# Memory laid out transposed, multiplied before it is normalised, in the opening of an encoder block on one core

## The reference, cut to what matters

```python
h = rms_norm(x, norm_mix_pre)               # 512 x 1024
z = h @ w_in                                # k, v, q, qx, pin, gates
mkv = rms_norm(mem, norm_mem) @ w_mem_kv    # 256 x 1024 @ 1024 x 1024
mk, mv = split(mkv)                         # keys and values, 4 heads of 128 columns each
ox = memory_attention(qx, mk, mv)
# rms_norm(x, g) = x * rsqrt(mean(x*x) + 1e-6) * g
```

## Time and profile before

| | before |
|---|---|
| median of 3 runs | 829.38 us (828.52 to 830.69) |
| span of the profiled execution | 827.4 us |
| granted TensorE clock, mean | 0.996 |
| instructions | 10167 |
| busy: PE / DVE / ACT / POOL | 816.6 / 353.0 / 304.7 / 40.0 us |

### The profile page before, as it was taken

The page is one execution under the profiler, slowest core; times in us unless marked ns, Lnnn a source line. Parts: engine busy times, 40 slices in busy tenths (PEclk is TensorE's granted clock), DMA queues, the critical chain, the costliest instruction groups (busy, mean ns, idle before and its releaser), DMA issues.

```text
span 827.4 us, 10167 instructions
## 1 busy us (share of the span) xinstructions
PE 816.6 (99%) x3952; PEld 673.3 (81%) x3952; DVE 353.0 (43%) x516; ACT 304.7 (37%) x574; POOL 40.0 (5%) x96
## 2 busy tenths in 40 slices
PE   7999999999999999999999999999999999999997
PEld 6988777777788888888888988888888888888885
DVE  4742565566344522525655443333333333522122
ACT  5742555555445324334334242233222332412110
POOL 1100000243000000000001000000000000000000
PEclk9999999999999999999999999999999999999999
DMA  9543221311311333334271133333322232622011
GB/s 322 168 129 109 74 79 52 103 52 51 103 51 51 103 102 103 101 102 147 107 254 52 51 102 102 101 101 101 97 82 82 93 126 102 244 80 84 1 51 51
DMA packets 67782, 84.16 MB, mean 102 GB/s; under 512 B 3217, under 2 KB 61089, under 8 KB 67746
## 3 DMA queue, kind: packets, MB, share of 16 engines
q1 hardware_dynamic: 67712, 83.65, 30.9%
q10 hardware_dynamic: 34, 0.01, 0.0%
HBM read 81.54 MB, written 2.11 MB: 101 GB/s over the span
## 4 chain that ended last, share of the span: by engine, by line
PE 97%; DMA 1%; DVE 1%; ACT 0%; issue 0%; SPq 0%; DVEq 0%; POOLq 0%; POOL 0%; ACTq 0%
PE pair L988 90%; PE pair L1079 1%; PE pair L1062 1%; PE pair L1089 1%; PE pair L994 1%; PE pair L1069 1%; PE pair L1093 1%; DMA g_mem_b<-in_norm_mem 1%; PE pair L1015 0%; DVE mem_in L738 0%; PE pair L1110 0%; DVE wo_lo L351 0%; ACT wo_hi L346 0%; PE pair L1100 0%; PE pair L1141 0%
## 5 line engine op out<-in xcount | busy, mean ns | idle before, releaser
L988 PE MATMUL pair<-h2T_hi,w_hi 128*128 128x512 f32 (+1 forms) x384 | 142.7, 372 | 0.0
L988 PE MATMUL pair<-h2T_lo,w_hi 128*128 128x512 f32 (+1 forms) x384 | 142.6, 371 | 0.0
L988 PE MATMUL pair<-h2T_hi,w_lo 128*128 128x512 f32 (+1 forms) x384 | 142.6, 371 | 0.0
L988 PE MATMUL pair<-hT_hi,w_hi 128*128 128x512 f32 x336 | 136.5, 406 | 0.0
L988 PE MATMUL pair<-hT_lo,w_hi 128*128 128x512 f32 x336 | 131.3, 391 | 0.0
L988 PE MATMUL pair<-hT_hi,w_lo 128*128 128x512 f32 x336 | 131.3, 391 | 0.0
L351 DVE TENSOR_TENSOR w_lo<-raw,w_hi 128x1024 fp32r<-128x1024 f32 x69 | 84.3, 1222 | 97.1 <-ACT w_hi L346 96.9
L346 ACT ACTIVATE w_hi<-raw 128x1024 fp32r<-128x1024 f32 x70 | 73.9, 1055 | 90.7 <-PE pair L988 89.3
L701 ACT ACTIVATE w_hi<-raw 128x1024 fp32r<-128x1024 f32 x40 | 42.4, 1061 | 147.3 <-PE pair L988 147.3
L950 DVE TENSOR_TENSOR w_lo<-raw,w_hi 128x1024 fp32r<-128x1024 f32 x40 | 49.0, 1226 | 85.5 <-ACT w_hi L701 85.5
L988 PEld LDWEIGHTS pair<-h2T_hi,w_hi 128*128 128x128 f32 x384 | 72.3, 188 | 12.6
(11 more groups left out here) (151 smaller groups left out, 1089.1 us busy)
## 6 DMA issues: line engine op xcount, KB each, us to landing
raw<-in_w_in SPq DMA_DIRECT2D x42, 512.0 KB, 4.7
raw<-in_w_ffn_gate SPq DMA_DIRECT2D x22, 512.0 KB, 4.7
raw<-in_w_ffn_up SPq DMA_DIRECT2D x22, 512.0 KB, 4.8
raw<-in_w_ffn_down SPq DMA_DIRECT2D x22, 512.0 KB, 3.7
raw<-in_w_mem_kv SPq DMA_DIRECT2D x8, 512.0 KB, 7.0
raw<-in_w_branch_a SPq DMA_DIRECT2D x8, 512.0 KB, 4.1
raw<-in_w_out SPq DMA_DIRECT2D x8, 512.0 KB, 4.1
x_in<-in_x SPq DMA_DIRECT2D x4, 512.0 KB, 9.7
```

What stands on the lines that cost most here:

```text
L988: ins = pe.matmul(dst, a, b, start=first and n == 0, stop=last and n == 2)
```

## The change

- The memory arrives transposed (`mem_t`, [128, 8, 256]: contraction down the partitions), its gain as a column per slice (`g_mem_c`), issued first on ScalarE's queue. The broadcast load of the gain, the two squares, the two normalisations and the 16 transposes of the memory are gone.
- ScalarE writes `memT_hi` as memory times gain, slice by slice of the contraction, VectorE `memT_lo`; the first weight slice is split in two halves between them. Step 0's matmuls wait slice by slice.
- 1/rms is found beside the steps: GpSimd squares the transposed memory and adds the eight slices to one (`mem_sum_of_squares`), a tile `mem_sum` at the end of step 2 adds over the partitions with a matmul against 1/D, VectorE adds eps, GpSimd takes the power (ahead of x block 2's).
- The memory steps run values first (4, 5, 6, 7, 0, 1, 2, 3). A tile `mem_scale` at the end of step 4 spreads 1/rms over the partitions (ones times a diagonal, which `mem_diagonal` writes on VectorE in iteration 4). Keys are evicted by VectorE, multiplied by it; values are multiplied by 1/rms as they leave PSUM for `mv`.
- Loads: memory half 0, weight half 0, memory half 1, weight half 1, chunk 1, x blocks 0 and 1, chunk 2, x blocks 2 and 3. The x blocks are squared and normalised in iterations 2 to 5 instead of 0 to 3, and turned behind steps 3, 4, 5, 6 instead of 2, 3, 5, 6.
- TensorE begins with 12 transposes, the two spreads, and 28 transposes, instead of 30, the memory's turns, and two spreads with 3 each.

```diff
@@ -63,8 +46,9 @@
-WARM_UP = (30, 0, 3)
-X_AFTER = (2, 3, 5, 6)
+WARM_UP = (12, 28)
+X_AT = 2
+X_AFTER = (3, 4, 5, 6)
 TAIL = 8
@@ -86,7 +70,7 @@
-    steps = [[("mem", h)] for h in range(2 * X_HEADS)]
+    steps = [[("mem", h)] for h in (4, 5, 6, 7, 0, 1, 2, 3)]
     steps += [[("k", 0)], [("v", 0)]]
@@ -102,6 +86,8 @@
+    steps[2].append(("mem_sum", 0))
+    steps[4].append(("mem_scale", 0))
     first = steps.index([("pin", 0)])
@@ -397,27 +399,35 @@
+            def load_half(c, h, signal):
+                src, dst = chunk_halves(stream[2 * c])[h], raw[c % 2][:, h, :]
+                if len(src.shape) == 3:
+                    dst = dst.rearrange("p (k n) -> p k n", k=4)
+                sp.dma_start(dst, src).then_inc(signal, 16)
             def load_chunk(c):
...
                     sp.wait_ge(weights_split, 2 * c - 2)
-                for h, src in enumerate(chunk_halves(stream[2 * c])):
-                    dst = raw[c % 2][:, h, :]
-                    if len(src.shape) == 3:
-                        dst = dst.rearrange("p (k n) -> p k n", k=4)
-                    sp.dma_start(dst, src).then_inc(raw_in[c % 2], 16)
-            for m in range(MT):
-                sp.dma_start(mem_in[:, m, :], mem[P * m:P * m + P, :]).then_inc(mem_loaded[m], 16)
-            sp.dma_start(g_mem_b[:, :], row_bcast(g_mem)).then_inc(gain_loaded["mem"], 16)
-            load_chunk(0)
+                for h in range(2):
+                    load_half(c, h, raw_in[c % 2])
+            def load_x(t):
+                sp.dma_start(x_in[:, t, :], x[P * t:P * t + P, :]).then_inc(x_loaded[t], 16)
+            for h, signal in enumerate((half_in, raw_in[0])):
+                sp.dma_start(memT_in[:, 4 * h:4 * h + 4, :], mem_t[:, 4 * h:4 * h + 4, :]).then_inc(mem_loaded[h], 16)
+                load_half(0, h, signal)
             load_chunk(1)
-            for t in range(TT):
-                sp.dma_start(x_in[:, t, :], x[P * t:P * t + P, :]).then_inc(x_loaded[t], 16)
+            load_x(0)
+            load_x(1)
+            load_chunk(2)
+            load_x(2)
+            load_x(3)
             for half in range(2):
...
             sp.dma_start(scale_p[:, :], pool_scale).then_inc(smalls_loaded, 16)
-            for c in range(2, 6):
+            for c in range(3, 6):
                 load_chunk(c)
@@ -492,7 +503,27 @@
-            for n in range(MT + TT):
+            def mem_sum_of_squares():
+                for h in range(2):
+                    pool.wait_ge(mem_loaded[h], 16)
+                    v = memT_in[:, 4 * h:4 * h + 4, :]
+                    link(pool.tensor_tensor(mem_sq[:, 4 * h:4 * h + 4, :], v, v, ALU.mult))
+                for n in (4, 2, 1):
+                    ins = pool.tensor_tensor(mem_sq[:, 0:n, :], mem_sq[:, 0:n, :], mem_sq[:, n:2 * n, :], ALU.add)
+                    if n > 1:
+                        link(ins)
+                    else:
+                        ins.then_inc(mem_summed, 1)
+            mem_sum_of_squares()
+            for n in range(TT):
+                if n == 2:
+                    pool.wait_ge(tile_merged, merged_no[("mem_sum", 0)])
+                    for m in range(MT):
+                        c = NORM_MEM + m
+                        pool.tensor_tensor(rstd[:, c:c + 1], meansq[:, c:c + 1], minus_half[:, :], ALU.pow)\
+                            .then_inc(mem_rstd_ready, 1)
                 inverse_rms(n)
@@ -619,16 +650,18 @@
                 for h in range(2):
-                    turn_hi(E_MEM + 2 * t + h)
-            for m in range(MT):
-                act.wait_ge(mem_loaded[m], 16)
-                mean_square(mem_in[:, m, :], NORM_MEM + m, square0[:, :])
-            for m in range(MT):
-                for h in range(2):
-                    turn_hi(2 * m + h)
-                split_hi(act, m)
+                    turn_hi(2 * t + h)
+            act.wait_ge(gain_loaded["mem"], 16)
+            for h, (loaded, n, done_hi) in enumerate(((half_in, 16, half_hi), (raw_in[0], 16, weights_hi))):
+                act.wait_ge(mem_loaded[h], 16)
+                for k in range(4 * h, 4 * h + 4):
+                    act.activation(memT_hi[:, k, :], memT_in[:, k, :], ACT.Copy, scale=g_mem_c[:, k:k + 1])\
+                       .then_inc(mem_hi_done, 1)
+                act.wait_ge(loaded, n)
+                ks = slice(4 * h, 4 * h + 4)
+                act.activation(split_at(0)[0][:, ks, :], raw_view(0)[:, ks, :], ACT.Copy).then_inc(done_hi, 1)
+            split_hi(act, 1)
             act.wait_ge(gain_spread, 2)
@@ -651,9 +684,10 @@
                             take(t)
-                if s < TT:
-                    act.wait_ge(x_loaded[s], 16)
-                    mean_square(x_in[:, s, :], NORM_X + s, square0[:, :])
+                if X_AT <= s < X_AT + TT:
+                    t = s - X_AT
+                    act.wait_ge(x_loaded[t], 16)
+                    mean_square(x_in[:, t, :], NORM_X + t, square0[:, :])
                 if s - 1 in X_AFTER[:-1]:
@@ -829,21 +863,41 @@
+            def mem_evicted(t):
+                kind, i = t
+                n = tile_no[t]
+                src = bk(n % 4)
+                dve.wait_ge(tile_full, n + 1)
+                if kind == "mem_sum":
+                    c = NORM_MEM
+                    dve.tensor_scalar(meansq[:, c:c + MT], src[:, 0:MT], 1.0, EPS, ALU.mult, ALU.add)\
+                       .then_inc(tile_merged, 1)
+                elif kind == "mem_scale":
+                    dve.tensor_copy(mem_scale[:, :], src[:, 0:N_MEM]).then_inc(tile_merged, 1)
+                    dve.wait_ge(tile_merged, merged_no[t])
+                else:
+                    dve.tensor_tensor(mk[:, i, :], src[:, 0:N_MEM], mem_scale[:, :], ALU.mult).then_inc(tile_merged, 1)
+            def mem_diagonal():
+                for m in range(MT):
+                    dve.wait_ge(mem_rstd_ready, m + 1)
+                    dve.tensor_scalar(diag[:, m, :], ident[:, :], rstd[:, NORM_MEM + m:NORM_MEM + m + 1], None, ALU.mult)\
+                       .then_inc(diag_ready, 1)
             dve.wait_ge(gain_loaded["mem"], 16)
-            for m in range(MT):
-                norm_rows(mem_in[:, m, :], mem_in[:, m, :], NORM_MEM + m, g_mem_b[:, :])
-            turn_lo(0)
-            turn_lo(1)
-            dve.wait_ge(weights_hi, 1)
             hi, lo = split_at(0)
-            for h, signal in enumerate((half_split, weights_split)):
-                if h == 1:
-                    turn_lo(2)
+            for h, (hi_done, signal) in enumerate(((half_hi, half_split), (weights_hi, weights_split))):
+                for k in range(4 * h, 4 * h + 4):
+                    dve.wait_ge(mem_hi_done, k + 1)
+                    dve.scalar_tensor_tensor(out=memT_lo[:, k, :], in0=memT_in[:, k, :], scalar=g_mem_c[:, k:k + 1],
+                                             in1=memT_hi[:, k, :].bitcast(F32), op0=ALU.mult, op1=ALU.subtract)\
+                       .then_inc(mem_split, 1)
+                dve.wait_ge(hi_done, 1)
                 ks = slice(4 * h, 4 * h + 4)
...
                    .then_inc(signal, 1)
-            turn_lo(3)
             split_lo(dve, 1)
@@ -861,14 +915,19 @@
                     done += 1
-                if s < TT:
-                    norm_rows(x_in[:, s, :], x_in[:, s, :], NORM_X + s, g_mix_pre_b[:, :])
+                if X_AT <= s < X_AT + TT:
+                    t = s - X_AT
+                    norm_rows(x_in[:, t, :], x_in[:, t, :], NORM_X + t, g_mix_pre_b[:, :])
                 if s >= 1:
-                    for t in steps[s - 1]:
+                    for t in sorted(steps[s - 1], key=evict_order):
                         if t[0] == "map":
...
                             merge(t)
+                        elif t in merged_no:
+                            mem_evicted(t)
+                if s == 4:
+                    mem_diagonal()
                 if s - 1 in X_AFTER[:-1]:
@@ -884,10 +943,12 @@
                         if e < E_MV:
-                            dst = mv[:, e - E_X, :, :]
+                            c = NORM_MEM + e - E_X
+                            ins = dve.tensor_scalar(mv[:, e - E_X, :, :], as4(bk(4 + e % 4)), rstd[:, c:c + 1], None,
+                                                    ALU.mult)
                         else:
-                            dst = v_c[:, 4 * (e - E_MV):4 * (e - E_MV) + 4, :]
-                        dve.tensor_copy(dst, as4(bk(4 + e % 4))).then_inc(turned_split, 1)
+                            ins = dve.tensor_copy(v_c[:, 4 * (e - E_MV):4 * (e - E_MV) + 4, :], as4(bk(4 + e % 4)))
+                        ins.then_inc(turned_split, 1)
                 if 0 <= u < UNITS:
@@ -1014,6 +1075,18 @@
                     return
+                if kind == "mem_sum":
+                    pe.wait_ge(mem_summed, 1)
+                    for m in range(MT):
+                        ins = pe.matmul(dst[:, m:m + 1], mem_sq[:, 0, P * m:P * m + P], inv_d[:, :], start=True, stop=True)
```

(26 more changed lines are left out.)

58 lines of the change are left out of this document (34 added, 24 removed).

## The result

The changed kernel takes 836.88 us (median of 6 runs, 835.91 to 837.46) where the kernel before, on the same chip, takes 828.95 us. The ratio is 1.0089 (95% interval 1.0065 to 1.0113): 0.9% slower. The forecast was 826.8 us with a range up to 829.7. The profiled execution took 835.91 us and spans 833.9 us, 6.5 us more than the 827.4 of before.

A forecast was written before the change was run, and what follows sets the result against it. TensorE was taken as the bound. Step 0 4.7 us earlier, 0.8 us added work and the wait at mem_scale left the first x step 2.6 us earlier: 829.38 - 2.6 = 826.8 us, range 825.2 to 829.7.

The forecast's parts named there:

- The bound: Whole kernel: TensorE is busy for 99% of the span and holds 97% of the chain that ended last.
- the mark: Start of the first x step: work behind it is the same in both kernels, so its gain is the end's gain.
- k: Start of the first x step on TensorE: 42.85 us before the change, 40.27 us forecast, 2.6 us earlier.
- Part 1: The start, up to step 0: step 0 starts at about 10.1 us, 4.7 us earlier.
- rival (d): Ramp stays at the lower clock: step 0 at 14.7 us, 831.6 us; chance 0.12 with anything else slower or level.
- memory half 0 usable at about 4.1: First load in the new order: the memory's first half is usable at about 4.1 us.
- The 32-B packets: New load of the memory's gain column, 128 packets: taken at 0.2 us, between 0 and 0.8 us.
- Part 4: Edits at nothing: evictions, turns, load issues and GpSimd's squares (done by 15 us, VectorE keeping its 1.21 us) cost nothing.
- The argument against (d): Ramp's clock: in the earlier trace the transposes' spacing halved after only 3 us, when 13 of them had run.
- Part 2: TensorE's own work from step 0 to the first x step: 26.6 us plus 0.8 us for mem_sum and mem_scale.
- Part 3: New wait at mem_scale behind VectorE's queue and chunk 3's load: TensorE pauses 2.6 us, split of step 6 at 23.7 us.
- Rival (b): The clock falls again in the pause ahead of mem_scale: plus 1.4 us, 828.2 us; chance 0.22.

The follow-up runs named there:

- e5: The changed kernel with 30 transposes ahead of the spreads and 10 behind, instead of 12 and 28: 837.97 us, 1.0104 of the kernel before.
- e1: The changed kernel without GpSimd's squares and sums (sum preset to a constant, memory's sum of squares left out): 831.92 us, 1.0033 of the kernel before.
- e6: The changed kernel with the changes of e1 and e5 together: 832.24 us, 1.0045 of the kernel before.
- e8: The changed kernel with squares on ScalarE, sums on VectorE, e7's order, 30 and 10 transposes, x normalised one turn earlier: 826.79 us, 0.9977 of the kernel before.
- e12: e8 plus e10's halves, squares at s=1, sums behind a later split, x's turned halves ahead of the next normalisation: 825.10 us, 0.9958 of the kernel before.
- e10: The changed kernel with each half of the transposed memory contiguous in the source instead of interleaved: 835.05 us, 1.0073 of the kernel before.
- e2: The changed kernel with the memory's gain preset by a memset instead of loaded (gain left out): 836.15 us, 1.0076 of the kernel before.
- e7: e1 with mem_sum evicted and diagonals written in VectorE's turn s=3, and GpSimd's memory powers one block earlier: 828.46 us, 1.0002 of the kernel before.
- e4: The changed kernel with GpSimd's squares waiting for the split of the second weight slice: 834.29 us, 1.005 of the kernel before.
- e11: The changed kernel with e7's order alone, the squares staying on GpSimd: 832.05 us, 1.004 of the kernel before.
- e3: The changed kernel with GpSimd's squares and sums in 15 instructions of 256 columns instead of 5: 834.76 us, 1.0057 of the kernel before.

## Why the prediction was wrong

**The bound and the mark** were right: nothing behind k changed, and the span follows k's start in all thirteen kernels.

**Part 1, the start: wrong by 4.1 us.** Two things each hold step 0 near 14 us in the changed kernel, and the sum had neither. One is the clock of the ramp: the spreads took 3.75 us for the four matmuls instead of 2.1, and the 28 transposes 0.21 us each until 13.1 us instead of 0.109. This is rival (d), whose step 0 stood at 14.7 us. The other is VectorE's first low split, done only at 13.69 us behind GpSimd's squares. e5 takes the first away and starts step 0 at 13.84 us, released by that split; e1 takes the second away and starts at 13.97. With both gone it is 11.04 (e6), 9.79 (e8) and 10.07 us (e12). Of the eight kernels with 12 transposes ahead of the spreads, seven start step 0 at 13.81 to 14.19 us and one, e10, at 9.79. A third term was wrong too, "memory half 0 usable at about 4.1": ScalarE started on it at 5.99 us. The 32-B packets were taken at 0.2 us and cost about 0.6 (e2), inside their bounds; the layout of the source, 1.5 us (e10), was missed. This late load is hidden behind the ramp in step 0's start, and shows in chunk 2's issue (Part 4).

The argument against (d), that the spacing halved in the earlier trace rows when 13 transposes had run, took a moment at which the clock rose for a number that suffices. Two kernels limit what can be said of the cause. In e2 and e10 the 12 transposes and the spreads follow each other without a pause, the spreads from 4.84 and 4.81 us, and the four take 3.77 us in e2 and 2.02 in e10. So neither the count of transposes nor the 0.65 us of waiting for the gain row is the whole cause, and what is was not found.

The Trainium skill, "TensorE: Matmul & The Clock Gate", Part 1, says that the throttled state is the default and that activity releases it. The trace agrees in outline: the transposes start 0.21 us apart until 13.1 us and 0.11 us apart behind. The profile's granted clock says 1.00 for the whole ramp, so there the spacing has to be read, not the column.

**Part 2, TensorE's own work: right.** 26.6 + 0.8 us was predicted; e7 shows 27.54 without any wait. mem_sum takes 0.37 us and mem_scale 0.44 to 0.52 (0.35 and 0.45 predicted). "k would start at 37.5 us if nothing new waited": e12 with step 0 at 10.07 has k at 38.33, of which 0.6 us is a wait.

**Part 3, the pause at mem_scale: right in kind, too small.** There is one pause, released by VectorE's diagonal, behind the load of chunk 3, as described. One term was mis-sized and one left out. The split of step 6 started at 30.97 us instead of 23.7, since the chunk went out at 22.41 instead of 16 us; this follows from Part 4's error. And from the split's start to the diagonals' end the chain is 5.0 us, 4.9 predicted: right here, but partly by luck, since the sum had left out GpSimd's two powers of the memory, which stand ahead of x block 2's. In the changed kernel they are through in time; in e6, e1 and e4, where they run beside VectorE's low split and take 1.97 to 1.99 us, the chain is 5.9, 6.4 and 6.4 us. GpSimd's timeline:

```profile
31.46 1.07 POOL L525 TENSOR_TENSOR rstd<-meansq,minus_half 128x1 f32<-128x1 f32 x2 [1.47 <-DVE meansq L874]
33.42 0.19 POOL L499 TENSOR_SCALAR meansq<-part_meansq 128x1 f32<-128x1 f32 x1 [0.89 <-ACT square L568]
```

The memory's rstd is ready at 32.5 us, and the diagonals that use it are written at 35.48, because step 6's low split and x block 2's normalisation, with the square and the power that it waits for, stand ahead of them on VectorE. e7 and e11 move them forward and the pause is gone: it was a matter of the order, not of the load. The prediction took this order as given, since it had counted no rival without it.

Rival (b), the fallen clock, came true as well. Its price was 1.4 us, and it measures 1.5. It needs more than the pause's length: the clock fell behind pauses of 3.92 us and, in e1, 2.87 us, and in e11 behind pauses of 0.5 and 2.1 us in the ramp, but not behind 2.9 us in e4 or 2.8 us of before. What decides between them stays open.

**Part 4, the edits at nothing: the step that failed.** "7.8 us, but 2.22 us per 512 beside VectorE's two-input operations, which keep their 1.21 us". GpSimd's own end was right: the squares are done at 15.7 us (15 taken), and mem_sum doesn't wait for them in the changed kernel. VectorE does not keep its time. In the earlier trace rows VectorE's operation had started at 167.00, before GpSimd's at 167.14, so the row showed only the case in which VectorE is first, and it was read as both. Where GpSimd is first, VectorE loses up to 2.2 us an operation, 6.3 us in all. The squares were costed as a matter of when they end, with TensorE as the one who asks; the harm went through VectorE's queue, the weights' buffer and SP's queue, where chunk 2 left 7.2 us late. 5.4 us of that are the squares' (13.19 in e1); the rest is the late first loads (11.75 in e12, 11.3 taken). The squares give the 1.8 us in step 0, 1.05 of the 1.5 us by which the pause is longer, and 5 us of the time (e1). Where an expectation above speaks of more operations held up in the changed kernel, the count in its trace is five.

The page weighed there, "GPSIMD Engine Reference", section 1 of the Trainium skill, states the sharing of the SBUF interfaces with VectorE's instructions that have two SBUF inputs. That section names no loser. The runs show that it is whichever comes second: GpSimd's five operations take 8.7 us in the changed kernel and 10.8 in e4 (an estimate from the earlier trace rows is 7.8 alone), and VectorE waits for the GpSimd instruction in progress.

The rest of Part 4 held: TensorE never waits for the evictions of keys and values, and for the turned halves of x only in e8, e11 and e12, 0.2 to 1.0 us.

**The forecast as a sum.** The 9.12 us lie in the start (4.1), the two pauses (1.8 and 1.5) and the fallen clock (1.5), but these are places on TensorE's timeline and not prices. In e10 step 0 starts 4.4 us earlier and k 0.2 us earlier; e6 shows that without the squares, too, the early start moves little as long as mem_scale is late. What is priced by taking it away is the squares, 3.3 us of k, and the order, 4.4 us: together they bring k from 49.39 to 41.73 (e7). e6 is nearest to what the forecast assumed, no harm to VectorE and a ramp at the full clock, and its k at 45.01 is still 4.7 us behind 40.27. The high split of step 6 begins at 25.89 us, when chunk 3 has landed (25.8), where 23.7 was taken, 2.2 us; the chain behind it takes 5.9 us instead of 4.9, for the powers left out; and the clock falls, 1.5 us. So even without its failed step the forecast was short by these. That e1 comes to 46.13 us and 831.92 near rival (d)'s 45.0 and 831.6 is luck: (d) had 1.4 us of low clock in the first steps and none behind the pause, and took the chain as 4.9. Each rival had been priced against the forecast, none with another beside it.

## What to carry to other kernels

Before wide elementwise work goes to GpSimd "beside" VectorE, look at what VectorE does with two SBUF inputs in those microseconds, and follow its queue on to the buffers and loads that it releases; e8 and e12 put the squares on ScalarE and their sum on VectorE, between its splits, and no wait of more than 0.5 us ahead of mem_scale is left. A result that one matmul needs should be evicted, and its factors made, as soon as it is there and not at the end of a turn's queue: e7's change of order costs no instruction and is worth 2.6 to 4.8 us, by how it is measured (e7, e11). When a row is the evidence that an operation keeps its time beside another engine, see in that row which of the two started first.

## What was not expected of the hardware

- VectorE's operations with two SBUF inputs that start while GpSimd runs an elementwise instruction end a fixed time behind that instruction, which grows with their own columns: 0.28 us for 256 columns, 0.55 for 512, 1.08 for 1024 (e3, e4). So they seem to do all their work after it. 256 columns take 0.47 us alone and up to 2.11 us so (2.59 in e10), 512 columns 0.68 and 2.85 us. In pieces of 256 columns on GpSimd (e3) the excess is 0.3 to 0.55 us each. GpSimd waits in the same way for a VectorE operation that was first (0.61 and 1.60 us, e3).
- The first load of the kernel, 512 KB in 4 KB pieces whose source rows lie 8 KB apart, moves at 124 to 239 GB/s where a contiguous one moves at 332 to 409 (e10), and is through 1.5 us later. The second such load, 4 us on, moves at 356 to 430 GB/s.
- The stretch at the lower clock behind the pause at mem_scale is about 3.4 us long in the changed kernel, e1, e6 and e10, and 6.8 us in e2, e3 and e5; which of the two occurs was not settled.
- A 256-column copy of ScalarE with a scale per partition repeats every 0.40 us (four in 1.70 us), against the 0.26 us taken from the earlier trace rows for an eviction, which has no such scale and reads PSUM.
